# A two-block transformer kernel on one core: the first mixer's VectorE work moved to PSUM, ScalarE and GpSimd

## The reference, cut to what matters

```python
h = rmsnorm(x, g_mix[l])
proj = h @ w_in[l]
q_a, k_a, v_a, x_l, gate_l, q_m, gates = jnp.split(proj, offs, axis=-1)
q_a = partial_rope(q_a.reshape(b, s, ATTN_HEADS, HEAD_DIM), positions)      # 6 heads
k_a = partial_rope(k_a.reshape(b, s, ATTN_KV_HEADS, HEAD_DIM), positions)   # 2 heads
attn_out = windowed_gqa(q_a, k_a, v_a, attn_sink[l])                        # softmax with a sink
xc = centred_depthwise_conv(x_l, conv_w[l], conv_b[l])                      # 4 taps, 768 channels
lru_out = bidir_rglru(xc, ..., lru_lambda[l]) * jax.nn.gelu(gate_l)         # two scans over time
mem_out = memory_cross_attention(q_m, k_m, v_m)                             # 4 heads
g = jax.nn.sigmoid(gates + gate_b[l]).reshape(b, s, N_BRANCH, d)
merged = (g[:, :, 0] * (attn_out @ p_attn[l]) + g[:, :, 1] * (lru_out @ p_lru[l])
          + g[:, :, 2] * (mem_out @ p_mem[l]))
x = x + merged @ w_out[l]
```

## Time and the profile before

| | before |
|---|---|
| median of 3 runs | 2315.18 us |
| lowest, highest | 2309.21, 2315.8 us |
| the profiled execution, its own time | 2315.32 us |
| its span, first to last instruction | 2313.9 us |
| PE busy over the span | 2202.0 us (95%) |
| DVE, ACT, POOL busy | 1401.4, 1195.0, 869.1 us (61, 52, 38%) |
| mean granted TensorE clock | 0.988 |

### The profile page before, as it was taken

One profiled execution on the slowest core, in us unless ns is written; L12 is line 12 of the kernel. 1 busy time (PEld: TensorE's weight loads), 2 busy tenths in 40 slices (PEclk: granted clock), 3 DMA queues, 4 the chain that ended last, 5 costly groups with the idle time before them and its releaser, 6 DMA issues.

```text
span 2313.9 us, 38008 instructions
## 1 busy us (share of the span) xinstructions
PE 2202.0 (95%) x15186; PEld 2047.3 (88%) x15186; DVE 1401.4 (61%) x2409; ACT 1195.0 (52%) x2050; POOL 869.1 (38%) x477
## 2 busy tenths in 40 slices
PE   8888889999999979999999999999999999899999
PEld 7888879999999867888888799898998889899997
DVE  5758761586844597666665764446664665546664
ACT  6546434554444696554555355555444355555443
POOL 5555366687600392000003666460000766461000
PEclk9999999999999999999999999999999999999999
DMA  6443355555565404666665545355565554345555
GB/s 224 137 123 108 118 158 170 173 165 177 178 184 183 136 1 127 191 194 194 194 192 183 173 146 159 109 159 166 183 184 176 155 155 158 115 148 166 182 184 161
DMA packets 102930, 369.58 MB, mean 160 GB/s; under 512 B 11362, under 2 KB 13794, under 8 KB 102116
## 3 DMA queue, kind: packets, MB, share of 16 engines
q1 hardware_dynamic: 102756, 367.15, 51.4%
HBM read 364.49 MB, written 2.62 MB: 159 GB/s over the span
## 4 chain that ended last, share of the span: by engine, by line
PE 74%; DVE 17%; ACT 6%; issue 2%; DMA 1%; POOL 1%; SPq 0%; DVEq 0%; ACTq 0%
PE stream_bank L530 13%; PE stream_bank L531 13%; PE stream_bank L532 13%; PE side_bank L530 10%; PE side_bank L532 10%; PE side_bank L531 10%; DVE first_hot L1961 2%; DVE experts L1951 2%; ACT unit_hi L1046 1%; PE side_bank L592 1%; DVE unit_lo L1556 1%; POOL unit_lo L2284 1%; ACT squares L1072 1%; PE side_bank L611 1%; DVE hot L1919 1%
## 5 line engine op out<-in xcount | busy, mean ns | idle before, releaser
L2284 POOL TENSOR_TENSOR unit_lo<-raw,unit_hi 128x1024 fp32r<-128x1024 f32 (+1 forms) x305 | 744.6, 2447 | 445.1 <-ACT unit_hi L1046 444.6
L1046 ACT ACTIVATE unit_hi<-raw 128x1024 fp32r<-128x1024 f32 (+1 forms) x678 | 708.0, 1045 | 188.3 <-PE side_bank L532 92.9
L1556 DVE TENSOR_TENSOR unit_lo<-raw,unit_hi 128x1024 fp32r<-128x1024 f32 x373 | 459.4, 1232 | 403.4 <-ACT unit_hi L1046 403.0
L530 PE MATMUL stream_bank<-hT_hi,unit_hi 128*128 128x256 f32 x1672 | 494.0, 295 | 3.5 <-DVE unit_lo L1556 3.5
L531 PE MATMUL stream_bank<-hT_lo,unit_hi 128*128 128x256 f32 x1672 | 477.8, 286 | 0.0
L532 PE MATMUL stream_bank<-hT_hi,unit_lo 128*128 128x256 f32 x1672 | 477.6, 286 | 0.0
L530 PEld LDWEIGHTS stream_bank<-hT_hi,unit_hi 128*128 128x128 f32 x1672 | 325.7, 195 | 12.3 <-issue 6.3
L530 PE MATMUL stream_bank<-h2T_hi,unit_hi 128*128 128x256 f32 x1152 | 327.4, 284 | 2.6 <-DVE unit_lo L1556 2.5
L531 PEld LDWEIGHTS stream_bank<-hT_lo,unit_hi 128*128 128x128 f32 x1672 | 325.8, 195 | 1.6
L531 PE MATMUL stream_bank<-h2T_lo,unit_hi 128*128 128x256 f32 x1152 | 326.7, 284 | 0.0
L532 PE MATMUL stream_bank<-h2T_hi,unit_lo 128*128 128x256 f32 x1152 | 326.6, 284 | 0.0
(11 more groups left out here) (341 smaller groups left out, 4099.2 us busy)
## 6 DMA issues: line engine op xcount, KB each, us to landing
raw<-in_peer_u_dram SPq DMA_DIRECT2D x128, 512.0 KB, 3.6
raw<-in_peer_v_dram SPq DMA_DIRECT2D x128, 512.0 KB, 4.2
raw<-in_gate_dram SPq DMA_DIRECT2D x64, 512.0 KB, 3.6
raw<-in_gt_dram SPq DMA_DIRECT2D x44, 512.0 KB, 3.6
raw<-in_up_dram SPq DMA_DIRECT2D x44, 512.0 KB, 3.7
raw<-in_ffn_out_dram SPq DMA_DIRECT2D x44, 512.0 KB, 4.0
raw<-in_branch_dram SPq DMA_DIRECT2D x32, 512.0 KB, 3.7
raw<-in_w_gate_dram SPq DMA_DIRECT2D x24, 512.0 KB, 3.6
```

The lines of the kernel that those rows point to most:

```text
L530: mm(out, l.hi, r.hi, start=start, stop=False)
L1046: activation(k.unit_hi[n % SPLIT_SLOTS][:, 0:w], k.raw[n % RAW_SLOTS][:, 0:w], ACT.Copy).then_inc(k.sem("unit_hi"), 1)
L1556: V.tensor_tensor(k.unit_lo[s][:, 0:w], k.raw[n % RAW_SLOTS][:, 0:w], k.unit_hi[s][:, 0:w], ALU.subtract).then_inc(unit_lo, 1)
L2284: G.tensor_tensor(k.unit_lo[s][:, 0:w], k.raw[n % RAW_SLOTS][:, 0:w], k.unit_hi[s][:, 0:w], ALU.subtract).then_inc(k.sem("unit_lo_pool"), 1)
```

## The change

Seven edits, all within the first block's mixer and its `w_out`:

1. **Series on POOL.** After `z = 1/(ya + 2)` DVE signals `lam_inverse`; the rest of the series, 23 operations on 128x12, runs in a new side generator `tables` on POOL, which signals `rates`. ACT waits for `rates` ahead of the first gate.
2. **Short conv in PSUM.** The running sum of the four taps lies in half of bank `SIDE + 4`, and the last tap writes `xc` in SBUF. Since the gates' products use this bank, PE waits for all six blocks ahead of each of them.
3. **Rotation in PSUM.** The product with the sine stays in the bank, and the bank is freed by the sum; two banks (`SIDE + 2`, `SIDE + 3`) alternate. A chunk's sum comes after the next chunk's product with the sine. Heads wait for the banks' semaphores instead of `roped`.
4. **Gate products in PSUM.** For `p_attn` and `p_lru` the product is written back into the bank and then added to `total` from there, and the bank is freed after the sum.
5. **GELU at eviction.** The six `gl` units are evicted through ACT's GELU. `gelu_gate` does nothing more on DVE, and the six rounds that PE, ACT and DVE spent on it are gone, so every later step of `lru()` comes six rounds earlier relative to the weight stream.
6. **Heads normalised on ACT.** All ten heads of the mixer multiply `S` by the reciprocal on ACT, in the round after the exponential, as the second block's heads do.
7. **Half of the low halves on DVE at the end.** From `p_attn` 3 to `peer_q` 2 (24 units) every second low half is DVE's: 12 in place of 3.

The diff (context lines left out):

```diff
--- before.py
+++ after.py
@@ -269,7 +269,8 @@
-            by = "dve" if n % 8 == 0 or any(a <= n < b for a, b in alone) else "pool"
+            turns = 2 if U["p_attn", 0] + AHEAD <= n < U["peer_q", 0] + AHEAD else 8
+            by = "dve" if n % turns == 0 or any(a <= n < b for a, b in alone) else "pool"
@@ -615,10 +616,7 @@
-        if s.kind == "swa":
-            pe.wait_ge(k.sem("normed_act"), s.number - HEADS_MIXER + 1)
-        else:
-            pe.wait_ge(k.sem("normed"), s.number + 1)
+        pe.wait_ge(k.sem("normed"), s.number + 1)
@@ -660,7 +658,7 @@
-                pe.wait_ge(k.sem("lru_conv"), i + 1)
+                pe.wait_ge(k.sem("lru_conv"), LRU_BLOCKS)
@@ -687,8 +685,6 @@
-                    for i in range(LRU_BLOCKS):
-                        yield
@@ -698,7 +694,7 @@
-                bank = take(SIDE + 3, ("rope", c))
+                bank = take(SIDE + 2 + ROPE_ORDER.index(c) % 2, ("rope", c))
@@ -713,7 +709,7 @@
-            yield from pipeline([head(Head(k, "attn", h), [(k.sem("roped"), h + 3), k.over["va", 1]])
+            yield from pipeline([head(Head(k, "attn", h), [k.over["rope", h], k.over["rope", 6 + h // 3], k.over["va", 1]])
@@ -1101,11 +1097,10 @@
-        if s.kind == "swa":
-            act.wait_ge(k.sem("inverse"), s.number - HEADS_MIXER + 1)
-            for i, (a, kn) in enumerate(s.where):
-                last = activation(s.S[:, a:a + kn], s.S[:, a:a + kn], ACT.Identity, scale=s.den[:, i:i + 1])
-            last.then_inc(k.sem("normed_act"), 1)
+        act.wait_ge(k.sem("inverse"), s.number + 1)
+        for i, (a, kn) in enumerate(s.where):
+            last = activation(s.S[:, a:a + kn], s.S[:, a:a + kn], ACT.Identity, scale=s.den[:, i:i + 1])
+        last.then_inc(k.sem("normed"), 1)
@@ -1160,6 +1155,7 @@
+                    act.wait_ge(k.sem("rates"), 1)
@@ -1191,11 +1187,6 @@
-                    for i in range(LRU_BLOCKS):
-                        u = k.lru_t[:, 0, :]
-                        act.wait_ge(k.sem("gate_cubic"), i + 1)
-                        activation(u, u, ACT.Tanh, scale=float(np.sqrt(2 / np.pi))).then_inc(k.sem("gate_tanh"), 1)
-                        yield
@@ -1244,7 +1235,7 @@
-                evict("gl", i, k.gl[:, i, :])
+                evict("gl", i, k.gl[:, i, :], ACT.Gelu_apprx_tanh)
@@ -1258,7 +1249,7 @@
-                        act.wait_ge(k.sem("merged"), i + 1)
+                        act.wait_ge(*k.over[key, i])
@@ -1621,13 +1612,7 @@
-        if s.kind == "swa":
-            V.reciprocal(s.den, s.den).then_inc(k.sem("inverse"), 1)
-        else:
-            own.then(V.reciprocal(s.den, s.den))
-            for i, (a, kn) in enumerate(s.where):
-                last = V.tensor_scalar(s.S[:, a:a + kn], s.S[:, a:a + kn], s.den[:, i:i + 1], None, ALU.mult)
-            last.then_inc(k.sem("normed"), 1)
+        V.reciprocal(s.den, s.den).then_inc(k.sem("inverse"), 1)
@@ -1680,7 +1665,7 @@
-        yb, z, z2 = k.small("yb", 12), k.small("z", 12), k.small("z2", 12)
+        yb, z = k.small("yb", 12), k.small("z", 12)
@@ -1719,20 +1704,9 @@
-            own.then(V.reciprocal(z, z))
-            own.then(V.tensor_tensor(z, ya, z, ALU.mult))
-            own.then(V.tensor_tensor(z2, z, z, ALU.mult))
-            terms = 9
-            own.then(V.tensor_scalar(c8, z2, 1.0 / (2 * terms + 1), 1.0 / (2 * terms - 1), ALU.mult, ALU.add))
-            for i in range(terms - 2, -1, -1):
-                own.then(V.tensor_tensor(c8, c8, z2, ALU.mult))
-                own.then(V.tensor_scalar(c8, c8, 1.0 / (2 * i + 1), None, ALU.add))
-                if i % 3 == 0:
-                    yield
-            own.then(V.tensor_tensor(c8, c8, z, ALU.mult))
-            own.then(V.scalar_tensor_tensor(c8, c8, 2.0, yb, ALU.mult, ALU.add))
-            own.then(V.tensor_scalar(c8, c8, -LRU_C / 2, None, ALU.mult))
-            yield
+            V.reciprocal(z, z).then_inc(k.sem("lam_inverse"), 1)
+            for _ in range(4):
+                yield
@@ -1761,8 +1735,9 @@
-            V.scalar_tensor_tensor(t1[:, 0, :], t1[:, 0, :], 0.5, k.gl[:, i, :], ALU.mult, ALU.mult).then_inc(
-                k.sem("lru_gated"), 1)
+            if i == 0:
+                dve.wait_ge(*k.over["gl", LRU_BLOCKS - 1])
+            V.tensor_tensor(t1[:, 0, :], t1[:, 0, :], k.gl[:, i, :], ALU.mult).then_inc(k.sem("lru_gated"), 1)
@@ -1770,13 +1745,6 @@
-                yield
-            for i in range(LRU_BLOCKS):
-                gl = k.gl[:, i, :]
-                dve.wait_ge(*k.over["gl", i])
-                gelu_cubic(t1[:, 0, :], gl, "gate_cubic")
-                dve.wait_ge(k.sem("gate_tanh"), i + 1)
-                own.then(V.scalar_tensor_tensor(gl, t1[:, 0, :], 1.0, gl, ALU.add, ALU.mult))
@@ -1787,11 +1755,12 @@
-                own.then(V.tensor_scalar(xc, k.xl[:, i, 0:TOKENS], w(0), k.col("conv_b", i), ALU.mult, ALU.add))
+                sums = k.bank[SIDE + 4][:, i % 2 * TOKENS:(i % 2 + 1) * TOKENS]
+                own.then(V.tensor_scalar(sums, k.xl[:, i, 0:TOKENS], w(0), k.col("conv_b", i), ALU.mult, ALU.add))
-                    own.then(V.scalar_tensor_tensor(xc, k.xl[:, i, j:j + TOKENS], w(j), xc, ALU.mult, ALU.add))
+                    own.then(V.scalar_tensor_tensor(sums, k.xl[:, i, j:j + TOKENS], w(j), sums, ALU.mult, ALU.add))
-                V.scalar_tensor_tensor(xc, k.xl[:, i, j:j + TOKENS], w(j), xc, ALU.mult, ALU.add).then_inc(
+                V.scalar_tensor_tensor(xc, k.xl[:, i, j:j + TOKENS], w(j), sums, ALU.mult, ALU.add).then_inc(
@@ -1805,23 +1774,22 @@
+            turned = lambda i: k.bank[SIDE + 2 + i % 2][:, 0:TOKENS]
-                V.tensor_tensor(k.qk[:, c, :], k.qk[:, c, :], k.rope_tmp[:, :], ALU.add).then_inc(k.sem("roped"), 1)
-                dve.wait_ge(k.sem("roped"), i + 1)
+                V.tensor_tensor(k.qk[:, c, :], k.qk[:, c, :], turned(i), ALU.add).then_inc(k.free[SIDE + 2 + i % 2], 1)
-                if i:
-                    add(i - 1)
-                V.tensor_tensor(k.rope_tmp[:, :], k.bank[SIDE + 3][:, 0:TOKENS], k.rope_s[:, :], ALU.mult).then_inc(
-                    k.free[SIDE + 3], 1)
-                dve.wait_ge(*k.over["rope", c])
+                own.then(V.tensor_tensor(turned(i), turned(i), k.rope_s[:, :], ALU.mult))
+                if i:
+                    add(i - 1)
@@ -1861,12 +1829,16 @@
-                    gated_sum(gate, k.bank[k.bank_of[key, i]], (key, i), outs)
-                    total = k.gates[:, 2 * KD + i, :]
-                    if key == "p_attn":
-                        own.then(V.tensor_tensor(total, total, gate[:, 0, :], ALU.add))
+                    total, b = k.gates[:, 2 * KD + i, :], k.bank_of[key, i]
+                    product = k.bank[b][:, 0:TOKENS]
+                    if place == 0:
+                        gated_sum(gate, k.bank[b], (key, i), outs)
+                    else:
+                        dve.wait_ge(unit_mm, U[key, i] + 1)
+                        own.then(V.scalar_tensor_tensor(product, gate[:, 0, :], 1.0, product, ALU.add, ALU.mult))
+                        V.tensor_tensor(total, total, product, ALU.add).then_inc(k.free[b], 1)
+                        dve.wait_ge(*k.over[key, i])
-                        V.tensor_tensor(total, total, gate[:, 0, :], ALU.add).then_inc(k.sem("merged"), 1)
@@ -2318,8 +2290,27 @@
+        def tables():
+            yield from steps(5)
+            ya, yb, c8 = k.small("ya", 12), k.small("yb", 12), k.small("c8", 12)
+            z, z2, terms = k.small("z", 12), k.small("z2", 12), 9
+            pool.wait_ge(k.sem("lam_inverse"), 1)
+            own.then(G.tensor_tensor(z, ya, z, ALU.mult))
+            own.then(G.tensor_tensor(z2, z, z, ALU.mult))
+            own.then(G.tensor_scalar(c8, z2, 1.0 / (2 * terms + 1), 1.0 / (2 * terms - 1), ALU.mult, ALU.add))
+            for i in range(terms - 2, -1, -1):
+                own.then(G.tensor_tensor(c8, c8, z2, ALU.mult))
+                own.then(G.tensor_scalar(c8, c8, 1.0 / (2 * i + 1), None, ALU.add))
+                if i % 3 == 0:
+                    yield
+            own.then(G.tensor_tensor(c8, c8, z, ALU.mult))
+            own.then(G.tensor_scalar(c8, c8, 2.0, None, ALU.mult))
+            own.then(G.tensor_tensor(c8, c8, yb, ALU.add))
+            G.tensor_scalar(c8, c8, -LRU_C / 2, None, ALU.mult).then_inc(k.sem("rates"), 1)
-                     ("p_lru", KD)), [rope()])
+                     ("p_lru", KD)), [tables(), rope()])
```

## The result

The changed kernel takes 2292.35 us (median of 4 runs, 2289.47 to 2294.61), the kernel before 2315.34 in the runs beside it: a ratio of 0.9904, 95% interval 0.9892 to 0.9916, 23.0 us faster. The forecast was 2282.4, or 32.9 faster. The direction and the range held; a third of the gain is missing.

What follows compares the result with a forecast made beforehand. PE bounds the kernel, with at most 48.7 us of waits and lowered clock to win. Terms 3.6 + 3.8 + 6.3 + 10 + 3.7 + 1.5 + 4.0 = 32.9 off 2315.3 gave 2282.4 us, range 2268 to 2304.

Steps and rivals of the forecast that it cites:

- Series and conv: Series and short conv, 60 to 78 us: 5.1 us of stall and clock gone, 1.5 paid on PE, net 3.6.
- Memory heads: Normalising the memory heads on ACT: 4.3 us of stall and clock, 0.5 left, net 3.8.
- Gate sums: Expected sign in the changed profile: gate sums take 0.42 us, never 2.
- The lock: DVE operations with an operand in PSUM show no long form; those in SBUF alone meet POOL.
- attention, 10 forecast: Attention, 181 to 262 us: 17.1 us of stall and clock, residual 7, net 10.
- rotation, 6.3: GELU and rotation, 148 to 181 us: 8.8 us of stall, 2.5 left, net 6.3.
- rival C: Crowded middle: LRU shares rounds with rotation and attention, losing their 16.3 us; 2298.7, between 2294 and 2308; chance 0.18.
- Two signs of the list: Prediction wrong if first gate unit to last head stays over 105 us, or ACT idles on DVE's small operations.
- `p_mem` and `p_attn`: Stages after attention: net 3.7 us from the last pair's earlier reciprocals and scans, and 1.5 in `p_attn`.
- `p_lru` and `w_out`: Mixer's end: 5.7 us of waits for POOL's low halves, 1.7 left for loads, net 4.0.
- A: Whole kernel, terms as summed: 2282 us, between 2272 and 2294; chance 0.62.
- rival D: POOL's series stops the stream: 7.4 us for 1.5 and two clock drops, 9.3 worse, 2292; no separate chance.

Runs made afterwards that it cites:

- e8: The changed kernel with the series back on DVE; 2298.42 us.
- e4: The changed kernel with the LRU's product, forward scan, sum and product with `gl` going through a PSUM bank; 2284.59 us.
- e7: e4 without the LRU's long reciprocal on DVE, so the output is not the reference's; 2280.89 us.
- e6: e4 with a copy in place of the LRU's square root, so the output is not the reference's; 2278.98 us.
- e10: e4 with the head's 128x2 sum written as two operations of one tensor and one scalar a partition; 2283.03 us.
- e11: e4 with attention issued ahead of the LRU, e10's one-tensor sum and one empty round between the LRU's root and scans; 2287.51 us.
- e2: The changed kernel with the six empty rounds put back ahead of the LRU's first scans, GELU staying at the eviction; 2290.09 us.
- e9: The changed kernel with the gate products back in SBUF; 2295.70 us.
- e12: The changed kernel with only every eighth low half on DVE at the end of the mixer, as before; 2294.87 us.

## Why the prediction came out as it did

**Right.** *Series and conv*: 3.4 against 3.6, and 2.5 to 2.8 in the executions where the first gate waits, which the prediction had at nothing. POOL's small operations cost 0.20 to 0.25 us (23 of them, some 5 us, below the 8 that I took) and PE's waits for low halves there 1.0 (I had 1.5):

```profile
L2304 POOL TENSOR_SCALAR smalls<-smalls 128x12 f32<-128x12 f32 x8 | 1.9, 240 | 0.7
L2303 POOL TENSOR_TENSOR smalls<-smalls 128x12 f32<-128x12 f32 x8 | 1.7, 211 | 0.5
```

The clock is 1.00 where it was 0.91. The sentence that a late DVE would cost the first gate what it overruns was borne out by e8 (2.98). *Memory heads*: 3.0 against 3.8, one stall of 1.4 left instead of 0.5. *Gate sums*: 0.42, never 2. *The lock*, read off: with an input in PSUM no DVE operation was long in any of the 14 traces (760 to 832 of them in each, none over 0.70 us). "An operand in PSUM", as the prediction has it, is too wide, since an output there didn't help (e4's product, 2.80 us). The Trainium skill (SBUF — State Buffer, Who interferes with whom) states the lock for a DVE operation with two SBUF inputs, beside a GpSimd operation that reads SBUF, and names no size that is exempt. The trace agrees, with 128x2 numbers taking 1.44 us.

**The step that failed: attention, 10 forecast, and rotation, 6.3.** Together they gave 3.8. By waits and clock, rotation kept 4.8 + 1.7 of clock against the 2.5 that I left, and attention kept nearly everything: 11.9 of stall and 0.06 x 80 = 4.8 of clock, 16.7, where it had 17.1 before and I left 7. It is rival C's mechanism, at three quarters of its 16.3. Two signs of the list fired. From the first `gate` product (138.9) to the last head's product with v (251.1) it takes 112.2 us, over the 105 named (115.4 before by the same marks). And ACT idles on DVE's small operations, 11.0 us in six waits of the attention window:

```profile
ACT S L1102 <- DVE smalls L1615: 11.0, 6, 3.3
```

What was wrong is the way of reasoning. I argued from sums: DVE would have about 57 us of work (60.9 measured) in a stage of 68 to 70, so most stalls should go. (One reading of the trace before was off as well: of DVE's 29.6 us in the rotation's window 17.5 are the GELU's; 22 is all of its work, a part of which lies ahead of the window.) But a round is a chain: ACT's exponentials, DVE's sum and reciprocal, ACT's multiplication, PE's transposes. Each link is a short operation behind whatever stands ahead of it in a fixed list. There the LRU's scans stood (e4: 7.4 us), its reciprocal of 3.35 (e7: 4.7), the root's two table loads (e6: 3.6), the blocked sum (e10: 1.7), and the LRU's output that itself waits for ACT (e11). These prices don't add up to a remedy, since what is kept out of attention returns in `p_attn`.

**What made up for it: `p_mem` and `p_attn`, 8.5 against 5.2; `p_lru` and `w_out`, 6.1 against 4.0.** The first comes from the LRU's six rounds, shown by e2, which loses 7.0 of it, and not from the products' form (e9 loses none). So edit 5's earlier LRU, counted as a gain in `p_mem`, was the cause of most of the loss in the middle (9.6 of the missing 12.5 come back in e2); I had put the one at 3.7, the other at nothing apart from a residual. Of the second, 3.8 are the PSUM form (e9); the new share of the low halves, which the prediction counted on, adds nothing (e12), and no run attributes the other 2.3.

**The range held in part by luck.** Rotation and attention alone were 12.5 us short of the forecast, which would have put the time at 2294.9, in rival C's band. Gains of 5.4 more than forecast in the two last stages brought it back into A's. The number is also rival D's (2292), but not its mechanism: PE waited 1.0 us for POOL's low halves beside the series, not 7.4, and the clock stayed at 1.00.

**Left out of the sum: the table loads around the roots.** The two loads that the GELU adds, at 122 and 162 us, were hidden as forecast: PE has no wait beside either. But six more stand around the three roots in the mixer (five before), and the prediction had no term for them. Where a head's exponential follows the root they lie on its chain, here in the changed kernel:

```profile
184.22 1.06 ACT L1186 ACTIVATE lru_b<-lru_b 128x1024 f32<-128x1024 f32 x1 [0.47 <-DVE lru_i L1724]
...
185.30 1.28 ACT L1093 ACT_TABLE_LOAD   x1
...
186.59 0.51 ACT L1093 ACTIVATE S<-S,smalls 128x256 f32<-128x256 f32 x1
```

The root ends at 185.28, the load starts at 185.30 and the exponential at 186.59: a switch costs 1.3 us. The drain of about 1.38 us a switch that the Trainium skill adds (ScalarE: Activation LUTs, What ACT_TABLE_LOAD costs) does not show here.

**Open.** The 2.2 us lost behind the mixer: the code there is not changed, and its length varied by 6 us over 14 executions, so nothing follows from it. The clock's part in each stall was read from windows, and no run separated it. Whether an LRU cut into finer steps, a few operations a round, would keep both attention and `p_attn` free was not tried; e2 and e11 only say that moving it whole doesn't.

## What to carry to other kernels

Where engines follow fixed lists, work taken off an engine pays only if it stood ahead of something that another engine was waiting for: write down the chain of the round link by link, with what stands ahead of each link, and only then count busy time. A change that moves a block of work to an earlier stage should be costed in both stages, and read with marks in the stream rather than from the end time. And no size of a DVE operation with two SBUF inputs was small enough to be safe beside a long POOL pass here. An input in PSUM made it safe for next to nothing. A scalar in place of the second tensor did so only at one column; wider operations of that form could still be long.

## What the hardware showed that I had not expected

A sum of 128x2 numbers took 1.44 us beside a POOL pass and 0.15 without; as two one-column operations with a scalar 0.19 to 0.22 each, in 44 of 44, ten of them inside such a pass. The same kind of operation took up to 1.58 us at two columns and 2.49 at 256. A scan of 256 steps took 0.69 to 0.70 us with an input in PSUM, as in SBUF, and was never held up; a product with both inputs in SBUF that wrote to PSUM was, up to 2.80. POOL's operations on 12 columns took 0.20 to 0.25 us, near what its wider ones gave as a fixed part. And the stretch behind the mixer took from 1955.4 to 1961.4 us in 14 executions, a spread as wide as most of the effects measured here.
